# One norm sum by additions on VectorE, a gather in plain fp32, and a first sum placed between two vectors

## What is computed

```python
def rmsnorm(x, g):
    y = x32 * lax.rsqrt(jnp.mean(x32 * x32, axis=-1, keepdims=True) + EPS)
...
def trunk(...):
    for l in range(DEPTH):
        mod = cmod @ p['w_ada'][l] + p['b_ada'][l]
        h = rmsnorm(x, norm_g[l, 0]) * (1 + sc1) + sh1
        x = x + g1 * mixer(h)
        h = rmsnorm(x, norm_g[l, 1]) * (1 + sc2) + sh2
        x = x + g2 * hier_moe(h)
    y = rmsnorm(x, final_g)
...
def hier_moe(h, ...):
    g_star = jnp.argmax(hf @ w_rg + b_rg, axis=-1)        # each token has one group
    ...                                                    # top 2 of its 4 experts
    hid = silu(h @ w1) * (h @ w3); out = (hid * combine) @ w2
```

## Time and profile before

| | us |
|---|---|
| median of 3 executions | 2570.24 |
| lowest and highest | 2568.32, 2570.51 |
| the profiled execution, its own time | 2564.58 |
| its span, first to last instruction | 2563.1 |
| TensorE busy in it | 2350.8 |
| VectorE, ScalarE, GpSimd busy in it | 787.8, 433.1, 118.9 |
| mean granted TensorE clock | 0.937 |

### The profile page before, as it was taken

The page is one execution under the profiler, slowest core; times in us unless marked ns, Lnnn a source line. Parts: engine busy times, 40 slices in busy tenths (PEclk is TensorE's granted clock), DMA queues, the critical chain, the costliest instruction groups (busy, mean ns, idle before and its releaser), DMA issues.

```text
span 2563.1 us, 27135 instructions
## 1 busy us (share of the span) xinstructions
PE 2350.8 (92%) x10320; PEld 1653.3 (65%) x10321; DVE 787.8 (31%) x1748; ACT 433.1 (17%) x662; POOL 118.9 (5%) x193
## 2 busy tenths in 40 slices
PE   5999999796999999799798999999999969999996
PEld 3777777574678876676553736536357746887765
DVE  1234443415111111354643443434331051111112
ACT  2223332203100000211210211212111031000001
POOL 0000000001000000000011020020110010000000
PEclk8999999797799999899999999999999986999998
DMA  6344333430044443111035052260422200444420
GB/s 271 124 149 165 133 124 124 159 123 9 32 158 164 156 159 120 70 45 43 32 137 183 25 221 82 76 220 25 165 99 95 70 21 1 164 158 162 156 82 38
DMA packets 77787, 290.74 MB, mean 113 GB/s; under 512 B 8912, under 2 KB 8912, under 8 KB 76928
## 3 DMA queue, kind: packets, MB, share of 16 engines
q1 hardware_dynamic: 54432, 200.57, 22.4%
q0 software_dynamic: 23264, 88.88, 9.4%
HBM read 241.94 MB, written 47.48 MB: 113 GB/s over the span
## 4 chain that ended last, share of the span: by engine, by line
PE 80%; DVE 7%; DMA 7%; ACT 3%; issue 3%; DVEq 0%; SPq 0%; ACTq 0%; POOL 0%; POOLq 0%
PE ps L450 21%; PE ps L718 15%; PE ps L727 9%; PE ps L686 4%; PE ps L540 3%; PE ps L924 3%; DMA ring<-in_wstream 3%; PE ps L462 3%; PE ps L744 3%; PE ps L917 2%; DMA arena<-in_c 2%; PE ps L933 2%; PE ps L896 2%; DMA out_mc_s<-arena 2%; PE ps L494 2%
## 5 line engine op out<-in xcount | busy, mean ns | idle before, releaser
L450 PE MATMUL ps<-hT,ring 128*128 128x288 f32 x1792 | 453.6, 414 | 17.7 <-ACT hT L998 12.9
L450 PEld LDWEIGHTS ps<-hT,ring 128*128 128x128 f32 x1792 | 344.2, 194 | 115.8 <-issue 13.5
L718 PE MATMUL ps<-arena,ring 128*128 x2048 | 399.4, 356 | 0.0
L718 PEld LDWEIGHTS ps<-arena,ring 128*128 128x128 f32 x2048 | 386.8, 190 | 10.3 <-issue 8.9
L727 PE MATMUL ps<-ring,arena 128*128 128x512 f32 (+1 forms) x512 | 221.0, 592 | 0.0
L450 PE MATMUL ps<-arena,ring 128*128 128x288 f32 x768 | 188.4, 409 | 3.8 <-DVE arena L1895 3.7
L450 PEld LDWEIGHTS ps<-arena,ring 128*128 128x128 f32 x768 | 146.8, 191 | 45.3 <-DVE arena L1895 4.2
L727 PEld LDWEIGHTS ps<-ring,arena 128*128 128x128 f32 (+1 forms) x512 | 90.3, 176 | 125.3 <-issue 125.3
L917 PE MATMUL ps<-arena 128*64 128x512 f32 x256 | 122.7, 610 | 17.3 <-DMA arena<-in_c 16.5
L1593 DVE TENSOR_TENSOR arena<-ps,arena 128x224 f32<-128x224 f32 x64 | 25.1, 391 | 359.6 <-PE ps L718 359.6
L924 PE MATMUL ps<-arena,xT 64*128 64x512 f32 x256 | 118.7, 603 | 0.0
(11 more groups left out here) (373 smaller groups left out, 2331.7 us busy)
## 6 DMA issues: line engine op xcount, KB each, us to landing
ring<-in_wstream SPq DMA_DIRECT2D x376, 512.0 KB, 3.3
arena<-in_c POOLq DMA_DIRECT2D x64, 512.0 KB, 4.5
out_mc_s<-arena POOLq DMA_DIRECT2D x64, 512.0 KB, 3.9
arena<-in_hg POOLq DMA_DIRECT2D x8, 512.0 KB, 3.9
out_hg_s<-arena POOLq DMA_DIRECT2D x8, 512.0 KB, 4.9
out_mc_p<-arena POOLq DMA_DIRECT2D x16, 256.0 KB, 2.6
xT<-in_xT SPq DMA_DIRECT2D x1, 2304.0 KB, 17.0
x_dram<-xT POOLq DMA_DIRECT2D x1, 2304.0 KB, 9.0
```

Of the source, the lines that this page charges most:

```text
L450: mm = pe.matmul(ps[:, 2 * p + half, 0:TH], ring[:, r, c * P:(c + 1) * P], rhs(k)[:, TH * half:TH * (half + 1)], start=(k == 0), stop=(k = ...
L718: mm = pe.matmul(ps[:, 2 * p, 0:W], ring[:, r, c * P:(c + 1) * P], mo["hs"][:, c, bass.ds(at_g, W)], start=(c == 0), stop=(c == DC - 1))
```

## The change

- Norm sums: VectorE adds the eight squares into `hT[:, 0, :]` (seven additions, `add_square`, one signal `sq_sum` each), and TensorE takes one pair of matmuls with ones in place of eight pairs. In `gated` the addition for a tile follows the next tile's update; the last one follows at the end. The optional windows do the same.
- Start: `norm_sums(0)` moves ahead of `ada_rows` for the second vector on TensorE; on ScalarE `squares(0)` and the inverse root move ahead of the second vector's copy; on VectorE the additions stand between the two `modulation` calls.
- Gather: `h_hi`, `h_lo` and GpSimd's subtraction go. `h_tok` holds all five tiles in plain fp32, `P` is written as plain fp32, and the gather has five plain fp32 matmuls where it had ten in fp32r. The fifth tile's lower 64 rows are zeroed by a `memset` on VectorE, so that all matmuls there, also L671 and L696, take 128 rows.

```diff
-        h_hi, h_lo = (shaped(arena_r[:, at:at + TJ * D], TJ, D) for at in (y_at, y_at + TJ * D))
-        h_tok = shaped(mo["more_y"][:, 0:2 * D], 2, D)
-        P_r = shaped(arena_r[:, 0:TJ * TW], TJ, TW)
+        h_tok = shaped(arena[:, R_AT + y_at:R_AT + y_at + TJ * D], TJ, D)
...
-            def h_remainder(layer):
-                for j in range(TJ):
-                    m = P if j < 4 else 64
-                    pool.wait_ge(s["htok_ready"].sem, TJ * layer + j + 1)
-                    s["hlo_ready"].on(pool.tensor_tensor(h_lo[0:m, j, :], h_tok[0:m, j % 2, :], h_hi[0:m, j, :],
-                                                         ALU.subtract))
...
             def norm_sums(n):
-                for c in range(DC):
-                    pe.wait_ge(s["sq_ready"].sem, DC * n + c + 1)
-                    for half in range(2):
-                        mm = pe.matmul(ps[:, 6 + half, 0:TH], ones, hT[:, c, TH * half:TH * (half + 1)],
-                                       start=(c == 0), stop=(c == DC - 1))
-                s["ss_ready"].on(mm)
+                pe.wait_ge(s["sq_sum"].sem, DC * (n + 1))
+                s["ss_ready"].on(wide((6, 7), [ones], [hT[:, 0, :]]))
...
+            norm_sums(0)
             ada_rows(1, R, 2)
-            norm_sums(0)
             turn_ada_rows(1, 2)
...
-                pe.wait_ge(s["hlo_ready"].sem, TJ * (layer + 1))
+                pe.wait_ge(s["htok_ready"].sem, TJ * (layer + 1))
...
-                        for part in (h_lo, h_hi):
-                            for j in range(TJ):
-                                m = P if j < 4 else 64
-                                mm = pe.matmul(ps[:, 2 * p + half, 0:TH], part[0:m, j, P * c:P * (c + 1)],
-                                               P_r[0:m, j, TH * half:TH * (half + 1)],
-                                               start=(part is h_lo and j == 0), stop=(part is h_hi and j == TJ - 1))
+                        for j in range(TJ):
+                            mm = pe.matmul(ps[:, 2 * p + half, 0:TH], h_tok[:, j, P * c:P * (c + 1)],
+                                           mo["P"][:, j, TH * half:TH * (half + 1)], start=(j == 0), stop=(j == TJ - 1))
...
-            for n in range(2):
-                ada_rows(n, ada_slot(n) + DC)
+            ada_rows(0, ada_slot(0) + DC)
             act.wait_ge(x_in, 16)
             squares(0)
+            inverse_root(0)
+            ada_rows(1, ada_slot(1) + DC)
             norm(0)
...
-                    act.copy(h_hi[0:m, j, :].rearrange("p (a n) -> p a n", a=2), ps[0:m, b0:b0 + 2, :])
-                    if j >= 2:
-                        act.wait_ge(s["hlo_ready"].sem, TJ * layer + j - 1)
-                    s["htok_ready"].on(act.copy(h_tok[0:m, j % 2, :].rearrange("p (a n) -> p a n", a=2), ps[0:m, b0:b0 + 2, :]))
+                    s["htok_ready"].on(act.copy(h_tok[0:m, j, :].rearrange("p (a n) -> p a n", a=2), ps[0:m, b0:b0 + 2, :]))
...
+            def add_square(n, c):
+                dve.wait_ge(s["sq_ready"].sem, DC * n + c + 1)
+                if c == 0:
+                    dve.sem_inc(s["sq_sum"].sem, 1)
+                    s["sq_sum"].n += 1
+                else:
+                    s["sq_sum"].link(dve, tt(hT[:, 0, :], hT[:, 0, :], hT[:, c, :], ALU.add))
...
                     s["x_tile"].link(dve, tt(xT[:, m, TP:T], xT[:, m, TP:T], tmp, ALU.add))
+                    if m:
+                        add_square(n, m - 1)
+                add_square(n, DC - 1)
...
-            for n in range(2):
-                modulation(n)
+            modulation(0)
+            for c in range(DC):
+                add_square(0, c)
+            modulation(1)
...
+                dve.memset(h_tok[64:P, 4, :], 0.0)
...
-                    ins = ts(P_r[:, j, :], iota1, pos[:, j:j + 1], None, ALU.is_equal)
+                    ins = ts(mo["P"][:, j, :], iota1, pos[:, j:j + 1], None, ALU.is_equal)
```

More of the change, by code:

```diff
@@ L52 @@
 MORE = T // W
-X_PE, X_ACT, X_DVE = 6 + DC, E + 2, 5 * E + 2 + 4 * DC
+X_PE, X_ACT, X_DVE = 6 + DC, E + 2, 5 * E + 2 + 4 * DC + DC - 1
 EPS = 1e-6
@@ L263, in build @@
         names = (
-            "dve act num_full lb_in lb_out conv_acc silc_clear rsh_ready slot_used silc turned sq_ready ss_ready "
+            "dve act num_full lb_in lb_out conv_acc silc_clear rsh_ready slot_used silc turned sq_ready sq_sum ss_ready "
             "rstd_ready h_ready x_tile y_ready decay f_ready diffs exps elem_ready scored scored_s "
@@ L268, in build @@
             "htok_full htok_ready cS_full cS_ready pos_full pos_ready gathered ce_ready cb_full y_full "
-            "yg_ready scattered scaled pt_ready y_hi_ready hlo_ready ohg_ready hid_ready xm_ready "
+            "yg_ready scattered scaled pt_ready y_hi_ready ohg_ready hid_ready xm_ready "
             "bdv_ready xc_ready v_full v_read gates_full abs_ready soft_ready dec_ready dec_exp "
@@ L380, in further_weights @@
                     pool.wait_ge(x_dve[layer].sem, X_DVE * (k + 1))
-            h_remainder(0)
             pool.wait_ge(s["x_tile"].sem, 2 * DC)
@@ L421, in _ @@
             pool.dma_start(xT, io["x_dram"]).then_inc(x_back, 16)
-            h_remainder(1)
             pool.wait_ge(s["x_tile"].sem, 4 * DC)
@@ L668, in moe @@
                 for j in range(TJ):
-                    m = P if j < 4 else 64
                     dst = ps[:, 2, P * j:P * (j + 1)] if j < 4 else ps[:, 3, 0:64]
-                    mm = pe.matmul(dst, ones[0:m, :], dg[0:m, j, 0:m], start=True, stop=True)
+                    mm = pe.matmul(dst, ones, dg[:, j, 0:P if j < 4 else 64], start=True, stop=True)
                 s["pos_full"].on(mm)
@@ L694, in moe @@
                             for j in range(TJ):
-                                m = P if j < 4 else 64
-                                mm = pe.matmul(ps[0:NE, 4 + half, 0:TW // 2], comb[0:m, j, :],
-                                               P_r[0:m, j, TW // 2 * half:TW // 2 * (half + 1)].bitcast(F32),
+                                mm = pe.matmul(ps[0:NE, 4 + half, 0:TW // 2], comb[:, j, :],
+                                               mo["P"][:, j, TW // 2 * half:TW // 2 * (half + 1)],
                                                start=(j == 0), stop=(j == TJ - 1))
@@ L989, in squares, with inverse_root @@
                     s["sq_ready"].on(act.activation(hT[:, c, :], xT[:, c, :], ACT.Square))
-            def norm(n):
+            def inverse_root(n):
                 act.wait_ge(s["ss_ready"].sem, n + 1)
@@ L994, in norm @@
                 s["rstd_ready"].on(act.activation(rstd, rstd, ACT.Exp, scale=-0.5))
+            def norm(n):
+                if n:
+                    inverse_root(n)
                 if n < 2 * LAYERS:
@@ L1133, in further_windows @@
                         done.on(act.copy(xy[0:CH[1], 1, :].rearrange("p (a n) -> p a n", a=2), ps[0:CH[1], 6:8, :]))
-                        act.wait_ge(x_dve[layer].sem, X_DVE * (k + 1))
+                        act.wait_ge(x_dve[layer].sem, X_DVE * k + (5 * E + 2 + 4 * DC))
                         for c in range(DC):
@@ L1316, in norm @@
                                        ALU.mult, ALU.mult))
+            def add_square(n, c):
[5 more added lines that the diff above has]
+                    s["sq_sum"].link(dve, tt(hT[:, 0, :], hT[:, 0, :], hT[:, c, :], ALU.add))
             def gated(full, base, nslot, use, layer, k, tmp):
+                n = 2 * layer + k + 1
                 for m in range(DC):
@@ L1641, in further_windows @@
                             X.link(dve, tt(xT[:, m, TP:T], xT[:, m, TP:T], tmp, ALU.add))
+                        dve.wait_ge(x_act[layer].sem, X_ACT * (k + 1))
+                        for c in range(1, DC):
+                            X.link(dve, tt(hT[:, 0, :], hT[:, 0, :], hT[:, c, :], ALU.add))
             moe(0)
```

## The result

| | before | changed |
|---|---|---|
| median, executions of one comparison | 2569.28 us | 2493.43 us (4 executions, 2491.76 to 2499.15) |
| ratio of the two, 95% interval | | 0.971 (0.969 to 0.973) |
| the profiled execution, its own time | 2564.58 us | 2492.52 us |
| its span | 2563.1 us | 2491.0 us |
| TensorE busy in it | 2350.8 us | 2292.1 us |

The change saves 75.9 us on medians and 72.1 us between the two profiled executions; 68.2 us were predicted. The forecast of 2502 us was 8.6 us too high and its range holds the time.

A forecast was written before the change was run, and what follows sets the result against it. TensorE, busy nearly throughout, was taken as the bound. Gather 22.0, routing 15.4, norms 1 and 3 6.2, norms 2 and 4 15.8 and start 8.8 sum to 68.2 us, off the median 2570.24: 2502 us, range 2490 to 2517.

The forecast's parts named there:

- Gather: Gather and expert weights of both layers: 49.3 us against 60.26, 11.0 us a layer, 22.0 us saved; bounds 8.6 to 13.1 a layer.
- The cold start: Start of the gather at the low clock: 2.6 us extra, taken from norm 2; bounds 0.5 to 5 us.
- the fifth tile's extra 64 rows cost nothing that I count: Fifth tile in the gather: full 128-row matmuls add no time, since the price used comes from 128-row matmuls.
- The remark that at one and the same clock plain fp32 is dearer: Gather matmuls at full clock: two fp32r cost 0.27 us, one plain fp32 0.498; 21.6 us more a layer.
- The first rival: Clock stays low in the gather: 33.2 us longer a layer, the whole 2590 us; chance 5%.
- Routing: Before the gather: one copy a tile saves 2.4 us, the unstalled VectorE additions 5.3; both layers 15.4 us.
- The second rival: VectorE's stall in the routing stays or moves to other instructions: 10.6 us less gain, 2513 us; chance 8%.
- The new memset: Zeroing in the routing: falls where VectorE waits for TensorE's logits; without that cover 1.3 us a layer.
- Norms: Shorter TensorE sums: 6.2 us saved at norms 1 and 3, 15.8 at norms 2 and 4 (bounds 13 to 17).
- The rival that the sums don't shorten the norms: VectorE's additions or a loop's exit on ScalarE end last at norms 1 to 4: 22 us lost, 2524; chance 4%.
- Start: Norm 0 starts on VectorE at about 40.7 instead of 49.50: 8.8 us; second vector's four groups at 1.66 us each.
- The later freeing of slots: Second vector's slots free up to 6 us later, delaying the first head's loads; covered, otherwise some 3 us.

## Why the prediction was right, and where not

**Gather: the size right, the credit misplaced.** 22.0 us predicted, 23.6 found (12.8 and 10.8), within the bounds of 8.6 to 13.1 a layer. The price was right: 9.91/20 = 0.496 us for a plain fp32 matmul against 0.498, and 6.82 against 6.9 us for the experts' weights. The cold start was the mis-sized term in layer 0: 30.77 + 9.91 - 39.8 = 0.9 us instead of 2.6; in layer 1 it was 2.4. The step that fell short is "the fifth tile's extra 64 rows cost nothing that I count". They not only cost nothing, they save 6.1 to 7.7 us a layer, and in fp32r they alone lift the clock: 64.5 us by that one edit. The prediction says that the gain rests on the clock and on the 64-row matmul, but it put no price on the second. The remark that at one and the same clock plain fp32 is dearer was right, and it speaks for another change: fp32r on full tiles is 17.2 us a layer cheaper still. The rows for this stood ahead of the prediction: the last 40 fp32r matmuls at clock 1.00 took 210 ns each, while those of the scatter took 135. I priced with both and didn't ask where the 75 ns between them came from; on full tiles the same 40 took 137 ns each.

**The clock.** The first rival (clock stays low, 2590) did not occur; the clock was at 1.00 from 616 on, about 3 us into layer 0's gather, as forecast, and after some 6 us in layer 1's. Plain fp32 did lift it by itself, as the prediction argued, also with the 64-row matmul left in.

**Routing.** 15.4 predicted, 16.2 found. The fifth transposition begins 603.22 - 581.07 = 22.15 us behind Ln, where it was 24.86: 2.7 us (2.4 predicted). The four additions save 6.11 - 0.76 = 5.35 us (5.3). The spreading matmuls take 2.40 us instead of 2.69. The bounds had these 0.3 us down to a faster clock, but it was 0.50 in both; what went is the 64-row load there, ahead of which the weight loads had stood still for 0.22 us. The second rival (the stall stays) fell, and GpSimd was its cause. The new memset took 0.91 us and was covered: VectorE waited 1.42 us for TensorE behind it.

**Norms.** 6.2 predicted for norms 1 and 3, 2.7 + 3.5 = 6.2 found; 15.8 for norms 2 and 4, 8.4 + 9.0 = 17.4 found, a little above the bound of 17. The sums took the 2.2 us forecast (2.28), and gained 10.56 - 2.28 = 8.3 and 9.75 - 2.28 = 7.5, just the two terms. The excess at norm 4 is luck: it lies in the scatter ahead of it, 35.99 us before and 34.46 after by the clock alone. Behind the scatter's last matmul TensorE began the sums equally late, after 6.5 us before and 6.6 now. The rival that the sums don't shorten the norms fell.

**Start.** 8.8 predicted, 10.4 found at norm 0. Squares from 22.77 (23.0), additions to 29.58 (29.9), sums to 31.93 (32.1) came as forecast. Mis-sized was the second vector: its four groups took 5.46 us at once, not 4 x 1.66, because the clock rose to 1.00 at about 35.6 and the last third passed at that; the group of 1.66 us had run at 0.50 but for its last half microsecond. The later freeing of slots cost nothing that shows: TensorE's wait for the ring behind the first projection is 5.52 us, and 5.36 before.

**What was not in the sum.** The heads (-8.8), the mLSTM stage (+5.4) and layer 1's experts (+1.7) came in on no edit. For the heads the repeated executions show that they vary by as much, and the experts' 1.7 us went with the clock. The mLSTM stage took 866.1 us in both executions of the changed kernel and 867.8 to 871.6 us in the nine of the other kernels, with and without the change's parts; why it is shorter there stays open. Without the heads and the mLSTM stage the table's gains sum to 75.6 us, 7.4 us more than the sum of 68.2: 1.6 each at the gathers, at the start and at norms 2 and 4, 1.7 at layer 1's experts, 0.8 in routing. About 3 of the 7.4 (experts and scatter) are chance of these two executions. That 75.6 comes so near to the medians' 75.9 is therefore partly luck: one stage left out varies, and the other is unexplained. To subtract from the median was right, since the profiled execution of before was one with short heads; 2496 would have been nearer, because the terms together were too small.

## What to carry to other kernels

A matmul on 64 rows among matmuls on 128 cost more than it saved here, in fp32r and in plain fp32; 96 rows among 128, in the scatter, cost nothing that shows. Look for gaps in the weight loads around a smaller matmul, and where there are some, fill the rows with zeros if the data allow it. When a stretch runs at a low clock although TensorE counts as busy, compare one matmul's price there with the same matmul elsewhere at the same clock; a difference points to a second cause, and mending it may be the cheaper edit. And when a change has several parts in one place, ask of each what it would do alone: here the smallest one, two zeroing instructions, was worth most of the gain, and plain fp32 cost 30 us beside fp32r on the same full tiles.

## What the runs showed of the hardware

- In fp32r a 64-row weight load had idle time of 0.28 us before and 0.25 us behind it at the low clock; in plain fp32 0.39 and 0.38 at the full one. In fp32r, loads of 128 rows followed one another without a gap, and so did loads of 128 and 96 rows in turn in the scatter, at 0.135 us a matmul.
- TensorE counted as busy for the whole 43 us and was still granted 0.50 all that time; with the gaps closed the same matmuls were granted 1.00 after some 5 us, and with plain fp32 and the gaps left open after some 3 us in layer 0 and 9 in layer 1. The busy share of the page doesn't tell which of these will be granted the full clock.
- A VectorE addition of 20 elements a row takes 0.18 us, and 1.81 us beside GpSimd's subtractions.
- The same kernel's HGRN2 heads took 462.0 us in one execution and 470.3 in another, at mean clocks of 0.93 and 0.91.
